# Another job order, early pieces, decays on GpSimd and unread matmuls in the RWKV core of a hybrid decoder trunk

## The reference

```python
u = rmsnorm(h, norm_mix[0]);  h = h + rwkv7_time_mix(u, ...)     # the stretch of the change
u = rmsnorm(h, norm_ffn[0]);  h = h + swiglu(u, f_w1, f_w3, f_w2)
u = rmsnorm(h, norm_mix[1]);  h = h + retention_mix(u, ...)
u = rmsnorm(h, norm_ffn[1]);  h = h + moe_swiglu(u, m_router, m_w1, m_w3, m_w2)  # top 2 of 8
out = rmsnorm(h, norm_final)
```

```python
def step(S, inp):
    r_t, d_t, k_t, v_t, aa_t, bb_t = inp                 # aa = -kk, bb = kk * a
    sa = einsum('bhvk,bhk->bhv', S, aa_t)
    S = S * d_t[:, :, None, :] + sa[..., :, None] * bb_t[..., None, :] + v_t[..., :, None] * k_t[..., None, :]
    y = einsum('bhvk,bhk->bhv', S, r_t)
    return S, y
# y = groupnorm(y) * gn_w + gn_b + sum(r * k * r_k) * v;  out = (y * g) @ wo
```

## Time and profile before

| | us |
|---|---|
| median of three runs | 1591.27 |
| lowest, highest | 1591.18, 1594.28 |
| profiled execution | 1586.79 |
| its span | 1584.7 |
| TensorE busy in it | 1561.4 (99%) |
| DVE busy | 1238.3 (78%) |
| ScalarE busy | 973.7 (61%) |
| GpSimd busy | 67.0 (4%) |

### The profile page before, as it was taken

One profiled execution on the slowest core, in us unless ns is written; L12 is line 12 of the kernel. 1 busy time (PEld: TensorE's weight loads), 2 busy tenths in 40 slices (PEclk: granted clock), 3 DMA queues, 4 the chain that ended last, 5 costly groups with the idle time before them and its releaser, 6 DMA issues.

```text
span 1584.7 us, 24868 instructions
## 1 busy us (share of the span) xinstructions
PE 1561.4 (99%) x9653; PEld 1297.1 (82%) x9653; DVE 1238.3 (78%) x984; ACT 973.7 (61%) x814; POOL 67.0 (4%) x34
## 2 busy tenths in 40 slices
PE   9999899999999999999999999999999999999997
PEld 7778758888998888888888888888888888888885
DVE  7594667774764457989988988988988988988995
ACT  1522345553424446787777777777777777777774
POOL 0043300000000000020000000000000000000200
PEclk9999999999999999999999999999999999999999
DMA  9121259856445525999999999999999999999991
GB/s 317 59 89 30 83 239 366 327 191 231 160 162 197 199 109 184 408 408 385 403 385 362 396 383 364 391 401 353 391 399 351 389 398 354 390 385 360 404 416 63
DMA packets 78588, 470.75 MB, mean 297 GB/s; under 512 B 7860, under 2 KB 8244, under 8 KB 26932
## 3 DMA queue, kind: packets, MB, share of 16 engines
q1 hardware_dynamic: 67860, 442.13, 72.5%
q10 hardware_dynamic: 9504, 23.37, 3.9%
q0 software_dynamic: 1152, 4.19, 0.7%
HBM read 450.27 MB, written 19.40 MB: 296 GB/s over the span
## 4 chain that ended last, share of the span: by engine, by line
PE 93%; DVE 5%; ACT 1%; issue 1%; DMA 0%; POOL 0%; DVEq 0%; SPq 0%; ACTq 0%; POOLq 0%
PE ps L1638 90%; PE ps L2206 2%; DVE mem L1162 1%; PE ps L2198 0%; DMA h<-x 0%; PE ps L1657 0%; DVE mem L1137 0%; ACT mem L760 0%; DVE mem L1145 0%; DVE mem L1134 0%; POOL mem L619 0%; DVE mem L1230 0%; DVE workr L1046 0%; PE ps L1857 0%; ACT work L876 0%
## 5 line engine op out<-in xcount | busy, mean ns | idle before, releaser
L1638 PE MATMUL ps<-pairs_r,workr 128*128 128x512 f32 x2856 | 661.6, 390 | 0.6 <-DVE workr L1380 0.6
L1638 PEld LDWEIGHTS ps<-pairs_r,workr 128*128 128x128 f32 x2856 | 534.8, 188 | 112.2 <-issue 1.1
L1638 PE MATMUL ps<-workr 128*128 128x512 f32 x2024 | 483.4, 393 | 0.0
L1638 PEld LDWEIGHTS ps<-workr 128*128 128x128 f32 x2024 | 375.5, 188 | 77.2 <-DVE workr L1607 0.4
L1544 DVE TENSOR_TENSOR workr<-ring,workr 128x2048 fp32r<-128x2048 f32 x167 | 380.9, 2291 | 52.7 <-ACT workr L958 52.5
L1544 DVE TENSOR_TENSOR pairs_r<-ring,pairs_r 128x2048 fp32r<-128x2048 f32 x165 | 374.0, 2290 | 18.1 <-ACT pairs_r L958 16.2
L958 ACT ACTIVATE pairs_r<-ring 128x2048 fp32r<-128x2048 f32 x165 | 316.9, 1922 | 109.4 <-PE ps L1638 103.9
L958 ACT ACTIVATE workr<-ring 128x2048 fp32r<-128x2048 f32 x167 | 319.3, 1917 | 43.5 <-PE ps L1638 36.2
L1083 DVE TENSOR_TENSOR pairs_r<-ring,pairs_r 128x2048 fp32r<-128x2048 f32 x68 | 155.9, 2292 | 110.3 <-ACT pairs_r L722 108.9
L1638 PE MATMUL ps<-mem 64*64 64x64 f32 (+7 forms) x3064 | 197.7, 260 | 8.0 <-issue 2.6
L722 ACT ACTIVATE pairs_r<-ring 128x2048 fp32r<-128x2048 f32 x65 | 124.5, 1916 | 124.5 <-PE ps L1638 121.5
(11 more groups left out here) (238 smaller groups left out, 654.8 us busy)
## 6 DMA issues: line engine op xcount, KB each, us to landing
ring<-mstream SPq DMA_DIRECT2D x336, 1024.0 KB, 7.1
ring<-pstream SPq DMA_DIRECT2D x65, 1024.0 KB, 5.0
mem<-rstream SPq DMA_DIRECT2D x27, 512.0 KB, 8.3
sent<-work ACTq DMA_DIRECT2D x6, 1024.0 KB, 8.0
back<-work ACTq DMA_DIRECT2D x6, 1024.0 KB, 11.5
mem<-rstream SPq DMA_DIRECT2D x16, 256.0 KB, 3.4
work<-sent ACTq DMA_DIRECT2D x7, 512.0 KB, 7.8
back<-work ACTq DMA_DIRECT2D x7, 512.0 KB, 9.1
```

Of the source, the lines that this page charges most:

```text
L1638: ins = nc.tensor.matmul(*args, **kw)
```

## The change

1. A new `order` for the same jobs, with five new words in it that are no jobs with an eviction: I1, I2, I3 (the own part of X1, X2, X3) and P0, P1 (the state parts of Y0, Y1). They are issued by TensorE alone, where they stand; the job proper then adds the rest in the same slot.
2. The decays of the state, L1265 on DVE before, are made by GpSimd (`decayed_state`): the first behind the gate terms, the second behind the subtraction of the head means. The sum of S1 and S2 on DVE waits for the new semaphore `state_decayed`.
3. Matmuls whose result nobody reads (identity times identity, 128x128 fp32): 4 in front of W0.1, 2 in front of U1, 5 of U2, 7 of S2, 4 of G0, once the job's slot is free; and 4 among the 8 matmuls of each Z.
4. The output projection's second half waits for Y1's eviction in place of U3's.

```diff
@@ -349,6 +349,7 @@
         s_gq0 = sem("first_group_squared")
         s_gr0 = sem("first_group_reciprocal_root_ready")
         s_gg0 = sem("first_group_gated")
+        s_sg = sem("state_decayed")
...
@@ -410,18 +411,21 @@
...
-        order = """V0:2 V1:0 M0:1 N0:3 M1:2 V2:0 N1:1 W0.1:3 H0.1:2 V3:0 W0.2:1 Q0.1:3 H0.2:2 V4:0 W0.3:1 H0.3:2
...
-                   U1:2 Q2.0:0 H1.5:3 Y0:1 S1:2 Q3.0:0 H1.6:3 X2:1 Q3.1:2 U2:0 S2:3 X3:2 U3:3 G0:1 Y1:0 G1:1"""
+        order = """V0:2 V1:0 M0:1 N0:3 M1:2 V2:0 N1:1 W0.1:3 H0.1:2 V3:0 W0.2:1 H0.2:3 V4:2 Z0:0 W1.1:1 W0.3:3 H0.3:2
...
+                   H1.5:3 U1:0 P0:1 Y0:1 Q2.1:2 S1:3 Q3.1:0 H1.6:1 I2:2 X2:2 Q3.0:3 U2:0 S2:1 I3:2 X3:2 P1:3 U3:0
+                   G0:1 Y1:3 G1:1"""
         slot_of = {}
         for word in order.split():
             name, _, s = word.partition(":")
             c, _, n = name[1:].partition(".")
             slot_of[name[0], int(c), int(n or 0)] = int(s)
-        jobs = list(slot_of)
+        sequence = list(slot_of)
+        jobs = [j for j in sequence if j[0] not in "IP"]
         number = {j: n for n, j in enumerate(jobs)}
-        before = {j: next((i for i in reversed(jobs[:n]) if slot_of[i] == slot_of[j]), None) for n, j in enumerate(jobs)}
+        before = {j: next((i for i in reversed(sequence[:n]) if slot_of[i] == slot_of[j]), None)
+                  for n, j in enumerate(sequence)}
         first_in = (J_G + 3, J_G + 4, J_WA + 8, J_RB + 2)
@@ -644,8 +648,17 @@
             nc.gpsimd.tensor_tensor(gtok, gtok, gnw.unsqueeze(1).to_broadcast([P, TT, D]), ALU.mult).then_inc(s_cb, 1)
             y0 = yS[:, 0]
             y0f = y0.rearrange("p h v -> p (h v)")
+            def decayed_state(c):
+                for done in stored(("S", c, 0)):
+                    pool.wait_ge(*done)
+                nc.gpsimd.tensor_tensor(St[3], St[c], gC.rearrange("p (n c) -> p n c", c=NC)[:, :, c + 1:c + 2].to_broadcast(
+                    [P, NP, 64]), ALU.mult).then_inc(s_sg, 1)
+            decayed_state(0)
             pool.wait_ge(s_gm0, 1)
             nc.gpsimd.tensor_tensor(y0, y0, gsum.unsqueeze(2).to_broadcast([P, NH, HN]), ALU.subtract).then_inc(s_gc0, 1)
+            decayed_state(1)
             pool.wait_ge(s_gc0, 1)
             pool.wait_ge(s_cb, 2)
             pool.wait_ge(s_gq0, 1)
@@ -1258,11 +1271,8 @@
                     if c == 0:
                         V.tensor_copy(new, b3).then_inc(s_jd, 1)
                     else:
+                        v.wait_ge(s_sg, c)
                         V.tensor_tensor(new, St[3], b3, ALU.add).then_inc(s_jd, 1)
-                    if c < NC - 2:
-                        g = gC.rearrange("p (n c) -> p n c", c=NC)[:, :, c + 1:c + 2].to_broadcast([P, NP, 64])
-                        v.wait_ge(s_jd, count[j, "d"])
-                        link(V.tensor_tensor(St[3], new, g, ALU.mult))
                 elif j == ("G", 1, 0):
                     V.tensor_copy(ygT[:, 4:8, c * P:(c + 1) * P],
                                   jbank(j, 1).rearrange("p (k s) -> p k s", k=4)).then_inc(s_ygT, 1)
@@ -1817,6 +1827,19 @@
                                 right(i, odd, r, p_), start=True, stop=True)
                 return ins
+            def own_part(job):
+                slot_free(job)
+                c = job[1]
+                wait_stored(("Q", c, 0))
+                wait_stored(("Q", c, 1))
+                pe.wait_ge(s_uv, c + 1)
+                for hd in range(NH):
+                    to, p_ = rows_at(hd % 2, c % 2), hd // 2
+                    ins = M(jbank(job, hd % 2)[to, p_ * 64:(p_ + 1) * 64], Qm[c][:, place(hd), 0:64], UV[:, c, hd, :],
+                            start=(p_ == 0), stop=(c == 0), skip_group_check=True)
+                return ins
             def state_part(job):
                 slot_free(job)
@@ -1829,19 +1852,29 @@
                             M(jbank(job, x_)[o, p_ * 64:(p_ + 1) * 64], AR[r, p_, c, 1, :], St[c - 1][r, p_, :],
                               start=(p_ == 0), stop=False, skip_group_check=True)
-            for j in jobs:
+            unread = {("W", 0, 1): 4, ("U", 1, 0): 2, ("U", 2, 0): 5, ("S", 2, 0): 7, ("G", 0, 0): 4}
+            for j in sequence:
                 kind, c, n = j
                 if j == ("G", 1, 0):
                     pe.wait_ge(s_ygT, 2)
                     wait_stored(("X", 3, 0))
                     mixer_output(0)
-                    wait_stored(("U", 3, 0))
+                    wait_stored(("Y", 1, 0))
                     mixer_output(2, tiles=range(6))
                 if before[j] is None:
                     pe.wait_ge(s_pe, first_in[slot_of[j]])
-                if kind != "Y":
+                if kind == "P":
+                    state_part(j)
+                    continue
+                if kind == "I":
+                    own_part(j)
+                    continue
+                if kind != "Y" and not (kind == "X" and c):
                     slot_free(j)
+                for _ in range(unread.get(j, 0)):
+                    nc.tensor.matmul(jbank(j, 0)[:, 0:P], ident, ident, start=True, stop=True)
                 if kind == "V":
                     t, m = c // 4, c % 4
                     for k in range(KT):
@@ -1858,6 +1891,8 @@
                 elif kind == "Z":
                     pe.wait_ge(s_z, 2)
                     for p_ in range(NP):
+                        if p_ % 2:
+                            nc.tensor.matmul(jbank(j, 1)[:, 0:P], ident, ident, start=True, stop=True)
                         ins = M(jbank(j)[:, 2 * p_:2 * p_ + 2], fm(rT)[:, p_, c * P:(c + 1) * P],
                                 qc[:, Q_SEL:Q_SEL + 2], start=True, stop=True)
                 elif kind == "Q":
@@ -1886,14 +1921,9 @@
                     W_ = lambda i, odd, r, p_: sets[c][f"W{(n - 1) % 2}"][r, odd ^ i, p_, :]
                     ins = four_corners(j, H_, W_) if kind == "W" else four_corners(j, W_, H_)
                 elif kind == "X":
-                    wait_stored(("Q", c, 0))
-                    wait_stored(("Q", c, 1))
-                    pe.wait_ge(s_uv, c + 1)
-                    for hd in range(NH):
-                        to, p_ = rows_at(hd % 2, c % 2), hd // 2
-                        ins = M(jbank(j, hd % 2)[to, p_ * 64:(p_ + 1) * 64], Qm[c][:, place(hd), 0:64], UV[:, c, hd, :],
-                                start=(p_ == 0), stop=(c == 0), skip_group_check=True)
-                    if c:
+                    if c == 0:
+                        ins = own_part(j)
+                    else:
                         wait_stored(("S", c - 1, 0))
                         for hd in range(NH):
                             to, r, p_ = rows_at(hd % 2, c % 2), rows_of(hd), hd // 2
@@ -1901,8 +1931,6 @@
                                     start=False, stop=True, skip_group_check=True)
                 elif kind == "U":
                     up = slice(64 * (1 - c % 2), 64 * (1 - c % 2) + 64)
-                    if c == NC - 1:
-                        state_part(("Y", 1, 0))
                     wait_stored(("H", c // 2, LEVELS))
                     wait_stored(("X", c, 0))
                     for hd in range(NH):
@@ -1918,8 +1946,6 @@
                         ins = M(jbank(j, 0)[r, p_ * 64:(p_ + 1) * 64], BKT[:, p_, c, r], UV[:, c, hd, :],
                                 start=True, stop=True)
                 elif kind == "Y":
-                    if c == 0:
-                        state_part(j)
                     wait_stored(("U", 2 * c + 1, 0))
                     for hd in range(NH):
                         p_ = hd // 2
```

More of the change, by code:

```diff
@@ L411, in build @@
         J_K, J_T1, J_G1, J_SS, J_RA, J_WA, J_RB, J_G, J_END = 0, 4, 5, 7, 11, 13, 21, 23, 27
-        order = """V0:2 V1:0 M0:1 N0:3 M1:2 V2:0 N1:1 W0.1:3 H0.1:2 V3:0 W0.2:1 Q0.1:3 H0.2:2 V4:0 W0.3:1 H0.3:2
-                   V5:3 W1.1:0 W0.4:1 H1.1:2 Z0:3 V6:0 H0.4:1 W1.2:2 V7:3 W0.5:0 H1.2:1 Z1:2 H0.5:3 Q0.0:0 Q1.0:1
-                   W1.3:2 H0.6:3 B3:0 X0:1 B1:2 H1.3:0 B2:3 B0:1 W1.4:2 U0:0 Q1.1:3 H1.4:1 S0:2 Q2.1:0 X1:3 W1.5:1
-                   U1:2 Q2.0:0 H1.5:3 Y0:1 S1:2 Q3.0:0 H1.6:3 X2:1 Q3.1:2 U2:0 S2:3 X3:2 U3:3 G0:1 Y1:0 G1:1"""
+        order = """V0:2 V1:0 M0:1 N0:3 M1:2 V2:0 N1:1 W0.1:3 H0.1:2 V3:0 W0.2:1 H0.2:3 V4:2 Z0:0 W1.1:1 W0.3:3 H0.3:2
+                   V5:0 H1.1:1 W0.4:3 V6:2 H0.4:0 W1.2:1 Z1:3 H1.2:2 W0.5:0 H0.5:1 V7:3 W1.3:2 Q0.0:0 H1.3:1 Q0.1:3
+                   Q1.0:2 H0.6:0 X0:1 W1.4:3 B1:2 Q1.1:0 B2:1 H1.4:3 B0:2 U0:0 W1.5:1 B3:3 I1:2 S0:0 Q2.0:1 X1:2
+                   H1.5:3 U1:0 P0:1 Y0:1 Q2.1:2 S1:3 Q3.1:0 H1.6:1 I2:2 X2:2 Q3.0:3 U2:0 S2:1 I3:2 X3:2 P1:3 U3:0
+                   G0:1 Y1:3 G1:1"""
         slot_of = {}
```

## The result

| | before | after |
|---|---|---|
| median, ten runs each | 1591.22 us | 1595.35 us |
| profiled execution | 1586.79 us | 1593.62 us |
| its span | 1584.7 us | 1591.5 us |
| TensorE busy in it | 1561.4 us | 1570.9 us |

The changed kernel is 0.27% slower: the ratio of the runs is 1.0027, with a 95% interval of 1.0015 to 1.0040.

The account below looks back on a forecast made before the run. TensorE, 93% of the chain, bounds the kernel. 6.6 (unread) + 3.5 (Z0) - 5.3 (waits gone) + 0.5 (waits left) + 0.5 (seams) = 5.8, rounded to 5.5; the median 1591.3 becomes 1596.5 us, range 1590.5 to 1602.

Parts of the forecast that it names:

- Unread matmuls: In the RWKV core, 30 matmuls with unread results add 0.22 us each to TensorE: +6.6 us.
- seams: TensorE loses about 0.15 us at each change of job shape, from unread groups and scattered pieces: +0.5 us taken.
- The wait at Z0: Z0, now right behind V4, waits on TensorE for DVE's bonus products, ending at 122.11 us: +3.5 us.
- Waits gone, -5.3, and left, +0.5: All 5.3 us of TensorE's core waits for engines go; 0.5 us comes back, with one eviction per job in the last chain.
- within 1 us: The tail from S1 to the output matmuls stays as long as it is, within 1 us, despite unread matmuls.
- Issue waits: TensorE waits in the core with no engine to blame, which follow no semaphore: unchanged at 2.6 us.
- The clock: Rival, 15%: the wait at Z0 drops TensorE to half clock, 1.9 us a spell: 1598.5 to 1600.5 us.
- no change by vanishing issue waits: Rival, 20%: unread matmuls let TensorE's queue fill, 2.6 us of issue waits go: 1593.5 to 1594 us.
- faster: Rival, 10%: DVE's bonus products get in before GpSimd's seeds and BKhat, so Z0 waits for nothing: 1587.2 us.
- late decay: Rival, 5%: GpSimd's decay comes late and S1 waits for it, +2 us: 1598.5 us.
- V7's end: V7, whose end releases the first output weights, ends 8 us later in the new order.
- The output weights: Loads for the output projection, started by V7's end, still land in time, with 3.5 us of slack: no cost.

Follow-up runs that it names:

- e2: The changed kernel without its 30 unread matmuls, order and GpSimd decays kept; 1590.66 us, ratio to before .9995.
- e4: The changed kernel with V5 moved in front of Z0 and no unread matmuls; 1587.12 us, ratio to before .9978.
- e8: As e4, with V6 also moved in front of W0.4 and the slots of V6 and H0.4 exchanged; 1586.07 us, ratio to before .9971.
- e6: The kernel before with the 30 unread matmuls added in its own order; 1590.07 us, ratio to before .9990.
- e7: The kernel before with the two state decays made by GpSimd, order and matmuls unchanged; 1591.11 us, ratio to before .9994.
- e10: As e8, with the two state decays back on DVE; 1589.22 us, ratio to before .9986.
- e1: The changed kernel with V5 moved in front of Z0, unread matmuls kept; 1591.41 us, ratio to before 1.0000.
- e3: The changed kernel with 14 more unread matmuls in front of Z0, nothing moved; 1592.14 us, ratio to before 1.0007.
- e5: The kernel before, unchanged, run and profiled a second time; 1591.12 us in one run.

## Why the prediction was right, and where not

The forecast was 1596.5 us with slower as the likeliest; it is 1595.35 and slower, 4.1 us over before. Term by term, for the profiled execution (5.8 by the sum, 6.8 measured):

- **Unread matmuls, +6.6, and seams, +0.5.** 60 records are 30 matmuls, 0.22 us each at full clock, and the group rows show 0.2 us more for each of the five groups: 7.6 us together, and e2 gives 7.6 gross. The balance of the other terms, 6.8 - 3.4 - 3.1 + 5.3 + 1.0, leaves only 6.6 for both. The missing 1.0 stands in no row of its own; e4 and e8 too are shorter than before by 0.2 and 1.0 us beyond what their waits explain, so it may lie in the new order. Wrong in what I left out: in the old order they about pay for themselves, with a higher clock (e6).
- **The wait at Z0, +3.5.** 3.4 us, L1175 its releaser. V4's last weight load was at 118.41 (forecast: end 118.7), Z0 began at 122.4 (122.2), and the products ended at 122.26 (122.11).
- **Waits gone, -5.3, and left, +0.5.** All 5.3 went and nothing came back. From the end of S1's sum to the row of the output matmuls it is 14.7 us (184.02 + 0.68 to 199.39), and was 14.6 (177.84 to 192.42): "within 1 us" held. The decay was half understood. I gave the whole 1.7 us before U2 to DVE's second decay; e7 shows that in the old order ScalarE's half of the copy would have held U2 for 1.0 of it, and e10 has 0.7 us before U2 and 1.6 us before U1, from the first decay, which I had given no wait. That the wait went whole here needs the order as well (Q3.0 behind X2).
- **Issue waits, 0.** -1.0 in this execution. They vary with the order without an edit aimed at them: 1.3 us (e2) to 5.1 (e7).
- **The clock, 0 in the sum and a rival at 15%.** This is the step that failed. One spell came, 3.1 us where the rival had 1.9 for one, and it came of the wait that the forecast itself contained (e1, e3). "Today the longest wait of TensorE is 1.7 us and the clock never falls" was true of the one execution that I read and not of the kernel: e5 has two spells. Both sides thus carry half-clock time. Runs of equal mean clock, averaged, compare so: at 0.996 before took 1589.5 us and after 1594.1, at 0.992 1594.4 and 1598.7. At equal clock the change costs 4.3 to 4.6 us.

That the median of 1595.35 came so near the forecast is luck: two errors met, a missed 3.1 us in after, and as many in ordinary runs of before (3.2 in e5), which I had called undisturbed. The 4.5 us between before's profiled execution and its median should have been the hint.

The Trainium skill, "TensorE: Matmul & The Clock Gate", section "HAM oscillation — how this bites in real kernels", says that a matmul kernel whose TensorE idles too long between bursts falls back to half clock and starts the next burst cold. Here the pair of after and e3 agrees (3.4 us of wait and a spell, 0.5 and none). That spell began at 124.30, 1.9 us after the wait had ended, and not with it; in e2 it was 0.3 us. Long gaps are not all of it here: e5 has spells behind waits of 1.3 and 2.0 us, and e10 one 2.5 us behind a wait of 0.16 us.

Of the rivals, "no change by vanishing issue waits" had 1.0 of its 2.6 us; "faster" failed where it said it would, L1175 starting at 109.65 behind L623; "late decay" failed with 9.5 us to spare (10 said). V7's end came 10.9 us later (153.32 against 142.42) where I had said 8; the spell, 3.1 us, stands before it. The output weights kept 5.7 us of slack at their use (199.05 + 2.8 against 207.6), where I had said 3.5.

What stays open: what the issue waits are. In the kernel before, the view of transfers from 100 to 140 us has one entry, eight packets of instructions, in the slices of 1 us at 100, 106, 110, 114, 122, 128, 131 and 138:

```profile
GB/s 16 0 0 0 0 0 16 0 0 0 16 0 0 0 16 0 0 0 0 0 0 0 16 0 0 0 0 0 16 0 0 16 0 0 0 0 0 0 16 0
...
q8 instruction: 8, 0.13, 1.2%
```

The packets at 106 and 128 us come some 2 us ahead of the issue waits that end at 108.66 and near 130.5; the others have none behind them. That TensorE waits for its instructions there is a guess; no experiment changed their number or place alone.

## What to carry to other kernels

Before unread matmuls are put in to hold the clock, look for real work that can stand in the wait: V5 in front of Z0 gave back 3.9 us, and then the fillers were worth taking out (4.3 us more at the median). Price a wait on the bound engine with what the clock does behind it, and profile the kernel before at least twice: one execution may be its best. An edit that takes work off an engine is to be tested in the order it will live in: the same one was worth nothing in one order, where another engine's half of the eviction came as late, and 2.8 us of waits in another (2.4 us of time, within the noise of two kernels).

## What was not expected of the hardware

- Spells at half clock came in lengths of 3.41, 6.83 and 10.24 us, at places that repeat within a few us over kernels (122 to 134, 185, 614 to 622 us) but not in every execution. The one near 620 us lies in a stretch that no kernel here touches; in before and after it was absent.
- 6.83 us at half clock cost 3.1 us, close to half, on work that is nearly all matmul; the mean clock of a whole run moves by 0.002 for it.
- DVE's first four bonus products took 9.89 us beside GpSimd and 1.66 without it, in before (10.53) and after alike.
